# Four slabs of a projection by Strassen's seven products, with the operand sums on GpSimd and VectorE

## The reference

```python
def _mixer_ab(h, w_in, a_qn, a_kn, b_qn, b_kn, b_sink, w_out):
    proj = jnp.einsum('bsd,de->bse', h, w_in)          # 256 x 1024 times 1024 x 2304
    qa, ka, va, qb, kb, vb = jnp.split(proj, AB_SPLITS, axis=-1)
    qa = _rmsnorm(qa.reshape(b, S, A_HEADS, HEAD_DIM), a_qn)
    ...
    oa = _dilated_mixture(qa, ka, va, slopes[0::2])
    ob, _ = _banded_attention(qb, kb, vb, B_WINDOW, B_BLOCK, 1.0, slopes[1::2], sink=b_sink)
    return jnp.einsum('bse,ed->bsd', concatenate([oa, ob]), w_out)
```

## Time and profile before

| | us |
|---|---|
| median of three runs | 622.19 (621.8 to 622.41) |
| the profiled execution | 622.04 |
| its span | 620.0 |
| TensorE busy | 570.4 (92%) |
| VectorE busy | 182.9 (30%) |
| ScalarE busy | 136.0 (22%) |
| GpSimd busy | 9.1 (1%) |

### The profile page before, as it was taken

One profiled execution on the slowest core, in us unless ns is written; L12 is line 12 of the kernel. 1 busy time (PEld: TensorE's weight loads), 2 busy tenths in 40 slices (PEclk: granted clock), 3 DMA queues, 4 the chain that ended last, 5 costly groups with the idle time before them and its releaser, 6 DMA issues.

```text
span 620.0 us, 9561 instructions
## 1 busy us (share of the span) xinstructions
PE 570.4 (92%) x3900; PEld 377.2 (61%) x3900; DVE 182.9 (30%) x591; ACT 136.0 (22%) x351; POOL 9.1 (1%) x25
## 2 busy tenths in 40 slices
PE   8999999998999969979999999999899996998897
PEld 7888876793554354344468876779355435345454
DVE  3334355253120110111036586415312010111101
ACT  3143546340011101101031357524001110100101
POOL 1100000000000000000002000000000000000000
PEclk9999999999999989998999999999999997999799
DMA  8999947498999999999999995529899999999996
GB/s 325 423 422 421 420 167 238 157 372 360 427 427 442 418 436 436 423 428 419 421 414 421 423 419 232 205 100 368 346 428 429 438 422 432 432 430 424 420 421 269
DMA packets 24242, 233.35 MB, mean 376 GB/s; under 512 B 2688, under 2 KB 3328, under 8 KB 6656
## 3 DMA queue, kind: packets, MB, share of 16 engines
q1 hardware_dynamic: 22176, 227.14, 88.2%
q10 hardware_dynamic: 2016, 5.52, 2.5%
HBM read 231.60 MB, written 1.05 MB: 375 GB/s over the span
## 4 chain that ended last, share of the span: by engine, by line
PE 70%; DMA 21%; issue 3%; DVE 3%; ACT 2%; ACTq 0%; DVEq 0%
DMA ring<-in_moe_w 20%; PE banks L813 15%; PE banks L1033 13%; PE banks L899 8%; PE banks L1007 7%; PE banks L1103 6%; PE banks L1119 5%; PE banks L859 2%; PE banks L788 2%; PE banks L887 2%; PE banks L876 2%; PE banks L1018 1%; PE banks L910 1%; PE banks L935 1%; DMA gains_xT<-in_xT 1%
## 5 line engine op out<-in xcount | busy, mean ns | idle before, releaser
L1033 PE MATMUL banks<-ring,desk 128*32 128x512 f32 x736 | 89.0, 624 | 9.2 <-DMA ring<-in_moe_w 9.1
L813 PE MATMUL banks<-ring,hT 128*128 128x256 f32 x416 | 94.6, 382 | 0.0
L813 PEld LDWEIGHTS banks<-ring,hT 128*128 128x128 f32 x416 | 77.3, 190 | 13.2 <-issue 3.6
L1328 ACT ACTIVATE desk<-banks 128x256 f32<-128x256 f32 x16 | 6.1, 383 | 273.6 <-PE banks L1033 273.6
L899 PE MATMUL banks<-heads,ring 128*128 128x256 f32 x256 | 61.9, 387 | 0.1
L1033 PEld LDWEIGHTS banks<-ring,desk 128*32 128x32 f32 x736 | 23.2, 114 | 60.7 <-issue 55.7
L1007 PE MATMUL banks<-desk,hT 128*128 128x128 f32 x384 | 49.3, 291 | 10.6 <-issue 10.6
L1007 PEld LDWEIGHTS banks<-desk,hT 128*128 128x128 f32 x384 | 48.9, 207 | 11.9 <-issue 11.4
L899 PEld LDWEIGHTS banks<-heads,ring 128*128 128x128 f32 x256 | 46.4, 190 | 12.6 <-issue 6.9
L1103 PE MATMUL banks<-ring,desk 128*32 128x512 f32 x400 | 46.2, 595 | 6.7 <-ACT desk L1330 5.7
L1119 PE MATMUL banks<-desk 128*128 128x256 f32 x224 | 52.1, 386 | 0.0
(11 more groups left out here) (180 smaller groups left out, 584.1 us busy)
## 6 DMA issues: line engine op xcount, KB each, us to landing
ring<-in_moe_w SPq DMA_DIRECT2D x66, 1024.0 KB, 27.1
ring<-in_moe_w SPq DMA_DIRECT2D x16, 4096.0 KB, 28.0
ring<-in_moe_w SPq DMA_DIRECT2D x17, 2048.0 KB, 11.6
ring<-in_ab_w_in SPq DMA_DIRECT2D x8, 1024.0 KB, 16.9
shared<-in_moe_w SPq DMA_DIRECT2D x8, 1024.0 KB, 7.1
shared<-in_moe_w SPq DMA_DIRECT2D x2, 4096.0 KB, 32.2
shared<-in_moe_w SPq DMA_DIRECT2D x3, 2048.0 KB, 13.0
ring<-in_c_w_in SPq DMA_DIRECT2D x5, 1024.0 KB, 20.3
```

The lines of the kernel that those rows point to most:

```text
L813: ins = pe.matmul(bank2(SLAB_BANK[layer][s], NT)[:, t, :], hT[:, c, t * P:(t + 1) * P], w[:, c, :], start=(c == 0 and t == 0), stop=(c == ...
L1033: ins = pe.matmul(bank(0)[j * SLOTS:(j + 1) * SLOTS, :], gathered_of(rd, place)[:, c, j * SLOTS:(j + 1) * SLOTS], w[:, j, :], start=(c == ...
```

## The change

Slabs 3 and 4, and slabs 6 and 7, are each computed as one 2x2 product of blocks: the tokens' two halves by the inner dimension's two halves, times the inner halves by the two slabs. Strassen's form (Winograd's variant) does that with seven block products and sums of blocks. A block product is four multiplications of the old shape.

- The four sums of token blocks are made once, by GpSimd (`add_tokens`), as soon as `hT` is complete. Four sums of weight blocks are needed for each pair: GpSimd makes those of slabs 3 and 4 (`add_weights(pool, G, 0)`), right behind, before its router preparations; VectorE makes those of slabs 6 and 7 (the step `weights`, behind `norm(1)`).
- These sums lie in three low slots of the ring, 16 to 18, which now take a unit only when slab 7 has been used. One sum of weights replaces a half of its slab in place.
- TensorE does the seven products of a pair in the order 1, 5, 6, 7, 2, 3, 4 (`product`). Products 1 and 2, 5 and 3, 7 and 4 are added by accumulating in PSUM. ScalarE copies products 1 and 5 and the first finished tile out; VectorE makes the other additions (`add_product`), with operands in PSUM but for one; ScalarE squares the finished tiles, now from SBUF.
- The list `ORDER_0` is rewritten around them.

```diff
+PAIRED = ((3, 4), (6, 7))
+SUMS_AT = 16
...
-    free = {s: (-1, None) for s in range(LOW)}
+    last = PAIRED[-1][1]
+    free = {s: (-1, None) if s < SUMS_AT else (last, last) for s in range(LOW)}
...
-            + each("turn", 0) + parts(3, 0) + each("turn", 1) + parts(3, 1)
-            + each("scores", 0) + parts(3, 2, 3) + each("normalise", 0) + parts(4, 0, 1)
-            + each("turn_prob", 0) + each("scores", 1) + parts(4, 2, 3) + each("prob_values", 0) + each("normalise", 1)
-            + parts(5, 0, 1) + each("norm", 1)
-            + each("turn_prob", 1) + parts(5, 2, 3) + each("turn", 3) + parts(6, 0) + each("turn", 4) + parts(6, 1)
-            + each("scores", 2) + each("prob_values", 1) + each("normalise", 2) + parts(6, 2, 3) + parts(7, 0)
-            + each("turn_prob", 2) + each("scores", 3) + parts(7, 1) + each("prob_values", 2)
-            + each("normalise", 3) + parts(7, 2, 3) + each("residual", 0) + each("norm", 2)
-            + each("turn_prob", 3) + parts(8, 0, 1) + each("prob_values", 3) + parts(8, 2, 3) + each("norm", 3)
+            + each("turn", 0) + products(0, 1) + each("turn", 1) + products(0, 5)
+            + each("scores", 0) + products(0, 6, 7) + each("normalise", 0) + products(0, 2, 3)
+            + each("turn_prob", 0) + each("scores", 1) + products(0, 4) + parts(5, 0)
+            + each("prob_values", 0) + each("normalise", 1) + parts(5, 1) + each("norm", 1) + each("weights", 1) + parts(5, 2)
+            + each("turn_prob", 1) + parts(5, 3) + each("turn", 3) + products(1, 1) + each("turn", 4) + products(1, 5)
+            + each("scores", 2) + each("prob_values", 1) + products(1, 6, 7) + each("normalise", 2) + products(1, 2)
+            + each("turn_prob", 2) + each("scores", 3) + products(1, 3) + each("prob_values", 2)
+            + products(1, 4) + each("normalise", 3) + parts(8, 0) + each("residual", 0) + each("norm", 2)
+            + each("turn_prob", 3) + parts(8, 1, 2) + each("prob_values", 3) + parts(8, 3) + each("norm", 3)
...
+        def add_weights(eng, unit, pair):
+            wa, wb = [ring_of(s).rearrange("p (c n) -> p c n", c=NC) for s in PAIRED[pair]]
+            b11, b21, b12, b22 = wa[:, 0:4, :], wa[:, 4:8, :], wb[:, 0:4, :], wb[:, 4:8, :]
+            t2, t3, t4 = [weight_sum[:, i, :, :] for i in range(3)]
+            for s in PAIRED[pair]:
+                unit_arrived(eng, s)
+            if pair:
+                pair_done(eng, pair - 1)
+            for i, (out, a, b) in enumerate(((t3, b22, b12), (b12, b12, b11), (t2, b22, b12), (t4, b21, t2))):
+                after(eng, s_wsum, 4 * pair + i)
+                unit.tensor_tensor(out, a, b, ALU.subtract).then_inc(s_wsum, 1)
...
+            def add_tokens():
...
+                pool.wait_ge(s_h, 4)
+                for i, (out, a, b, op) in enumerate(((s1, a21, a22, ALU.add), (s2, s1, a11, ALU.subtract),
+                                                     (s3, a11, a21, ALU.subtract), (s4, a12, s2, ALU.subtract))):
+                    after(pool, s_tsum, i)
+                    G.tensor_tensor(out, a, b, op).then_inc(s_tsum, 1)
+
+            add_tokens()
+            add_weights(pool, G, 0)
...
+                def multiply(out, a, b, start=False):
+                    for c in range(NC // 2):
+                        ins = pe.matmul(out, a[:, c, :], b[:, c, :], start=(start and c == 0), stop=(c == NC // 2 - 1),
+                                        skip_group_check=True)
+                    return ins
+
+                if j == 1:
...
+                elif j == 5:
+                    slab_taken(pe, 0, first - 1 if pair else 1)
+                    pe.wait_ge(s_tsum, 1)
+                    pe.wait_ge(s_wsum, 4 * pair + 2)
+                    multiply(y[:, 0, :], token_sum[:, 0, :, :], wb[:, low_half, :], start=True).then_inc(s_prod, 1)
+                elif j == 6:
+                    pe.wait_ge(s_p1, pair + 1)
+                    pe.wait_ge(s_tsum, 2)
+                    pe.wait_ge(s_wsum, 4 * pair + 3)
+                    multiply(x[:, 1, :], token_sum[:, 1, :, :], weight_sum[:, 0, :, :]).then_inc(s_prod, 1)
+                elif j == 7:
+                    pe.wait_ge(s_p5, pair + 1)
...
+                elif j == 2:
+                    pe.wait_ge(s_u, pair + 1)
...
+                elif j == 3:
+                    pe.wait_ge(s_v, pair + 1)
...
+                else:
+                    pe.wait_ge(s_wsum, 4 * pair + 4)
+                    multiply(y[:, 1, :], hT[:, high_half, rows_1], weight_sum[:, 2, :, :]).then_inc(s_used, 2)
...
+                if j == 6:
+                    product_done(dve, pair, 6)
+                    dve.wait_ge(s_p1, pair + 1)
+                    V.tensor_tensor(kept, kept, x[:, 1, :], ALU.add).then_inc(s_u, 1)
+                elif j == 7:
+                    product_done(dve, pair, 7)
+                    dve.wait_ge(s_u, pair + 1)
+                    V.tensor_tensor(widened, kept, y[:, 1, :], ALU.add).then_inc(s_v, 1)
...
+                    V.tensor_tensor(tile_of(second, 1), widened, fifth, ALU.add).then_inc(s_tiles, 1)
+                elif j == 4:
+                    pair_done(dve, pair)
...
+                    V.tensor_tensor(tile_of(first, 1), kept, y[:, 1, :], ALU.add).then_inc(s_tiles, 1)
+                    V.tensor_tensor(tile_of(second, 0), kept, y[:, 0, :], ALU.add).then_inc(s_tiles, 1)
```

More of the change, by code:

```diff
@@ L542, in parts, with products @@
             return [("slab", slab, part) for part in which]
+        def products(pair, *which):
+            return [("product", pair, j) for j in which]
         def rows(*pieces):
@@ L804, in slab @@
                     b = SLAB_BANK[layer][s]
-                    if b in SLAB_BANK[layer][:s]:
+                    pair = [i for i, (first, _) in enumerate(PAIRED) if layer == 0 and b in SLAB_BANK[0][first:s]]
+                    if pair:
+                        pe.wait_ge(s_c11, pair[-1] + 1)
+                    elif b in SLAB_BANK[layer][:s]:
                         slab_taken(pe, layer, max(k for k in range(s) if SLAB_BANK[layer][k] == b))
@@ L1139, in _ @@
                         slab(layer, i, part)
+                    elif what == "product":
+                        product(i, part)
                     elif what == "turn":
@@ L1170, in values_of @@
             def values_of(layer, s):
[L1172 removed]
+                _, _, first, _ = SLAB_PLAN[layer][s]
                 ps = bank2(SLAB_BANK[layer][s], NT)
[L1174 removed]
                 act.wait_ge(s_used, first_unit(layer, "in") + s + 1)
@@ L1177, in values_of @@
                 for t in range(NT):
-                    ins = A.activation(values[layer][:, t, first:first + cols.shape[-1]], cols[:, t, :],
+                    ins = A.activation(values[layer][:, t, first:first + 4 * HD], ps[:, t, :],
                                        ACT.Copy, scale=rstd[:, t:t + 1])
@@ L1201, in slab, with room_for, take_product @@
                              ACT.Square).then_inc(s_sqh, 1)
+            def room_for(s):
+                i = norm_slabs_before(0, s)
+                act.wait_ge(s_slab, i - 1)
+                act.wait_ge(s_hT_ps, turns_before(*NORMED[i - 1]))
+            def take_product(pair, j):
+                first, second = PAIRED[pair]
+                x, y = pair_banks(pair)
+                if j == 1:
+                    product_done(act, pair, 1)
+                    A.activation(kept, x[:, 0, :], ACT.Copy).then_inc(s_p1, 1)
+                elif j == 5:
+                    product_done(act, pair, 5)
+                    A.activation(fifth, y[:, 0, :], ACT.Copy).then_inc(s_p5, 1)
+                elif j == 2:
+                    product_done(act, pair, 2)
+                    room_for(first)
+                    A.activation(unnormed(0, first)[:, 0, :], x[:, 0, :], ACT.Copy).then_inc(s_c11, 1)
+                elif j == 4:
+                    act.wait_ge(s_c11, pair + 1)
+                    for k, s in enumerate((first, second)):
+                        kind = SLAB_PLAN[0][s][0]
+                        i = norm_slabs_before(0, s)
+                        w = 2 * HD if kind == "shared2" else 4 * HD
+                        act.wait_ge(s_tiles, 3 * pair + 2 + k)
+                        if kind == "shared2":
+                            act.wait_ge(s_rstd, 1)
+                            for t in range(NT):
+                                ins = A.activation(values[0][:, t, 512:512 + 2 * HD], late_tiles[:, t, 2 * HD:4 * HD],
+                                                   ACT.Copy, scale=rstd[:, t:t + 1])
+                            ins.then_inc(s_val, 1)
+                        act.wait_ge(s_slab, i - 1)
+                        A.activation(square[:, i % 2, 0:NT * w].rearrange("p (t n) -> p t n", t=NT), unnormed(0, s),
+                                     ACT.Square).then_inc(s_sqh, 1)
             def take_heads(layer, s, half):
@@ L1352, in _ @@
                         slab(layer, i)
```

(6 more changed lines are left out.)

67 lines of the change are left out of this document (60 added, 7 removed).

## The result

The changed kernel took 627.65 us (median of 6 runs, 626.16 to 628.13), the kernel before 621.91 us (6 runs, 621.5 to 622.41): a ratio of 1.0087, 95% interval 1.0074 to 1.0100. The forecast was 627.3 us. The profiled execution took 627.7 us, its span 625.7 us.

A forecast was written before the change was run, and what follows sets the result against it. TensorE was taken to bound the first mixer, whose shift reaches the end one to one: -3.5 (TensorE) + 5.5 (stall) + 2.4 (clock) + 0.7 (additions) = +5.1 us, giving 627.3 us; stated range 619.0 to 630.5 us.

The forecast's parts named there:

- TensorE's saving, -3.5 us: Two slab pairs in the first mixer: seven products replace eight, saving eight multiplications of 0.435 us, 3.5 us.
- GpSimd's sums, 2.2 us each: GpSimd's four weight sums of slabs 3 and 4: 2.2 us each, running from 21.8 to 30.9 us.
- The norm chain kept out: VectorE's norm of slabs 0 and 1 held out by GpSimd's sums: turn(0) at 33.6 us, TensorE stands 5.5 us.
- The router's multiplications, 1.0 us: GpSimd's two router multiplications, right behind the weight sums, delay VectorE's norm chain about 0.5 us each, 1.0 us.
- The clock, +2.4 us: Behind the 5.5 us stall at turn(0), TensorE's clock falls to 0.50 of 2.4 GHz, costing 2.4 us.
- The additions ahead of the normalisation, +0.7 us: Pair 1: VectorE's additions delay normalisation, so TensorE waits 0.4 us before turn_prob(2) and 0.3 us before turn_prob(3).
- VectorE's weight sums in pair 1, hidden: Four VectorE sums behind norm 1, 1.225 us each, 5.0 us together: hidden, with 0.6 to 0.8 us to spare.
- The reserved slots at 0: Ring slots 0 to 2 held for units 16 to 18: transfers stand about 10 us but catch up; cost 0.
- The shift of the mixer is the shift of the end: A first mixer ending later starts the saturated transfer stream equally later, so its shift reaches the end one to one.
- The forecast's own range: Whole kernel: 624.5 to 630.5 us, from sums of 1.9 to 2.6 us and clock loss of 0 to 2.9.
- the sums hide: Rival: VectorE's short norm instructions slip past GpSimd's sums, no stall; -3.5 + 0.7 gives 619.4 us; chance 0.27.
- A cheap stall: Rival: 1.67 us sums, stall at turn(0) 3.3 us, clock stays; +0.5, 622.7 us; chance 0.12.

The follow-up runs named there:

- vector_reordered: sums_on_vector with head 2's and 3's normalisations moved ahead of product 7's and 4's additions; 618.43 us, ratio 0.9913 to the kernel before; repeated, 618.72 us, 0.9941.
- router_later: Changed kernel, with GpSimd's router preparations waiting until norm(0) is done; 626.64 us, ratio 1.0047 to the kernel before.
- kept_busy: Changed kernel plus 24 dummy TensorE multiplications ahead of its wait at turn(0); 626.90 us, ratio 1.0056 to the kernel before.
- old_with_sums: Kernel before, plus eight unused GpSimd sums of the same sizes and the three reserved slots, no Strassen products; 629.09 us, ratio 1.0106.
- slots_only: Kernel before with only the three low slots held back until unit 7 is used; 621.66 us, ratio 0.9971; repeated, 621.67 us, 0.9990.
- sums_on_vector: Changed kernel, with VectorE making slabs 3 and 4's weight sums behind norm(0); 618.60 us, ratio 0.9941 to the kernel before; repeated, 619.07 us, 0.9946.
- sums_in_halves: Changed kernel, with each GpSimd weight sum of slabs 3 and 4 made in two instructions of 512 elements; 624.66 us, ratio 1.0018 to the kernel before.

## Why the prediction was right, step by step

**TensorE's saving, -3.5 us: right.** Pair 0 shows its half alone, 1.73 us from the first scores to `turn(3)`. For both pairs `vector_reordered` comes nearest: the waits of the change are gone, and its mixer is 3.40 and 3.42 us shorter.

**GpSimd's sums, 2.2 us each: 2.36 us.** The straight line through the short rows had said 2.33; the value taken below it was 7% low. A token sum is 1.26 to 1.28 us (four records of L801) where the line gave 1.25. The weight sums ran from 22.27 to 31.96 us, forecast 21.8 to 30.9: half of the difference is the unit, which landed later, half the length. The estimate from the Trainium skill, GPSIMD Engine Reference (3.1 Elementwise), 2.25 us, was 5% under.

**The norm chain kept out, `turn(0)` at 33.6 us, 5.5 us of stall: right in kind and nearly in size** (34.23 us, 5.61 us). One detail was off in the other direction: seven of the ten short ones were through when the last sum ended, not five. What came behind the sums therefore took 2.27 us instead of 2.7. TensorE also began slab 1 0.3 us later and was free at 28.6 us, not 28.1. That 5.5 and 5.61 us agree so closely is in part luck: a later and longer series of sums made the wait longer, fewer links left and a TensorE that asked later made it shorter. The Trainium skill, SBUF — State Buffer (SBUF: two separate sides), has the exclusive lock held for the whole instruction; the trace agrees, with 2.20 us for 16 elements beside sums of 2.36 us, and 1.12 us beside sums of 1.28.

**The router's multiplications, 1.0 us: 0.83 us**, from `router_later`.

**The clock, +2.4 us: 2.43 us in the trace**, and 2.34 us by `kept_busy`. From `turn(0)` to the first scores the loss is 1.4 us in `old_with_sums` after the same wait and 2.8 us in `router_later` after a shorter one. So the term has a spread of 1.4 us, more than the microsecond between the two rows that it was taken from the earlier trace rows. That the clock falls and costs time was forecast rightly; that the middle value hit is luck.

**The additions ahead of the normalisation, +0.7 us: 0.9 us.** The place was right, the two `turn_prob` rows are 0.34 us longer each; the rest is the wait for the first head ahead of them.

**VectorE's weight sums in pair 1, hidden: right.** They run from 61.06 us at 1.226 us each, and the scores of head 2 start without a wait behind them. **The reserved slots at 0: right**, by `slots_only` twice, though the transfers fall to a share of 0.55 from 60 to 75 us as foreseen, from 1.02.

**The shift of the mixer is the shift of the end: right.** Over 11 of the 14 traces the mixer varies from 95.5 to 106.5 us, and what is behind it only from 506.1 to 506.8. The three others have 0.9 to 2.2 us more, and I have no cause for it.

With the measured terms the sum is -3.5 + 5.6 + 2.4 + 0.9 = +5.4 us, the mixer shows +5.34, and the medians differ by 5.7. Two small pieces outside the forecast partly cancel: `turn(0)` comes 5.8 us later counted from slab 1's start, not 5.6, and behind 90 us the mixer has a shorter wait for VectorE (0.36 instead of 0.70 us).

**The range.** The forecast's own range, 624.5 to 630.5 us, isn't what its terms give: sums from 1.9 to 2.6 us and a clock loss of 0 to 2.9 us make 623.7 to 629.4 us. The measured 627.65 lies in both. The stated range, 619.0 to 630.5 us, holds faster and slower alike, so that it was met says little; what bears the forecast out is the chain of waits in the trace.

Of the rivals, "the sums hide" fell with the chain at 2.2 us a piece, though its price was right: the kernel in which they do hide, `sums_on_vector`, takes 618.60 and 619.07 us, where the rival said 619.4. "A cheap stall" is what the trace of `sums_in_halves` shows: 3.5 us without a fall of the clock in an execution of 622.42 us, where the rival said 3.3 us and 622.7 us. Its median is higher, 624.66 us (ratio 1.0018).

## What to carry to other kernels

Before giving an idle GpSimd some work, look at what VectorE does in the same microseconds: a chain of short two-input instructions pays one whole GpSimd instruction for every second link, and if TensorE stands at the end of that chain the price comes once as a wait and, where the clock falls during it (here after 4.39 us and more; in the one trace with a wait of 3.50 us it did not), once more as clock. Put such work where VectorE's chain is not on the path (here behind the norm, 3.5 us later), cut it into shorter instructions, or give it to VectorE itself behind the chain: 5.7 us of VectorE behind the norm cost TensorE no wait, 9.7 us of an idle GpSimd cost 8 us (5.6 of wait and 2.4 of clock).

## What the runs showed of the hardware

Not only two-input instructions were held. L1536, a `tensor_scalar` with one SBUF input of 16 elements, took 2.21 us beside a weight sum, and in the changed kernel the same one with 2 elements took 1.12 us beside a token sum, while the `tensor_reduce` of 512 elements at 22.94 us ran in its usual 0.69 us with a weight sum under way. The Trainium skill, SBUF — State Buffer (Who interferes with whom), says that `tensor_scalar` can enter a mode with two ports and that `tensor_reduce` never contends on trn2: the trace agrees with both.

Beside the weight sums the pattern is regular: a held VectorE instruction ends within 0.05 us of the end of a sum (31.99 and 31.96 us for the last), one of 0.17 us follows, and the next is held. The sums stand 0.08 us apart (9.69 us for four of 2.36). The router's two multiplications follow with no such gap (two of 0.66 us within 1.29), and beside them two VectorE instructions in a row are held, 0.59 us each. It goes both ways: in `sums_in_halves` GpSimd's eighth sum took 1.60 us instead of 1.28 beside VectorE's long multiplications.

TensorE's clock fell after waits of 5.61, 5.57 and 4.39 us, which cost 2.4, 1.4 and 2.8 us, and not after 3.50 us in the one trace of `sums_in_halves`. 24 multiplications of no use in the gap kept it at 2.4 GHz.
